# The opening and the close of a two-block transformer kernel rearranged: the conditioning row broadcast by TensorE, first chunk scaled from its bank, last sums by column halves

## The reference, cut to what matters

```
mods = silu(c) @ w_ada + b_ada               # nine rows of 1024: shift, scale, gate of three sublayers
n = rmsnorm(x, g_pre) * (1 + scale0) + shift0
f = (silu(n @ w_gate) * (n @ w_up)) @ w_down # D_FF = 2816, 22 blocks of 128 hidden units
h = x + 0.5 * gate0 * rmsnorm(f, g_post)
...                                          # attention, ffn1, second block with mlp0, MLA, mlp1
out = rms_norm(h + relu(hn @ w_up)**2 @ w_down, final_norm_g)
```

## Time and profile before

| | |
|---|---|
| time, median of 3 runs | 1213.88 us (1212.95 to 1217.24) |
| the profiled execution | 1212.7 us, its span 1211.4 us |
| PE busy | 1151.8 us, 95% of the span |
| DVE, ACT, POOL busy | 67%, 51%, 5% |
| mean granted PE clock | 0.988 |
| DMA | 231.75 MB, mean 191 GB/s |

### The profile page before, as it was taken

One profiled execution on the slowest core, in us unless ns is written; L12 is line 12 of the kernel. 1 busy time (PEld: TensorE's weight loads), 2 busy tenths in 40 slices (PEclk: granted clock), 3 DMA queues, 4 the chain that ended last, 5 costly groups with the idle time before them and its releaser, 6 DMA issues.

```text
span 1211.4 us, 19269 instructions
## 1 busy us (share of the span) xinstructions
PE 1151.8 (95%) x7570; PEld 1052.6 (87%) x7570; DVE 808.5 (67%) x1334; ACT 622.6 (51%) x1138; POOL 54.7 (5%) x75
## 2 busy tenths in 40 slices
PE   4999999899998999999999898999999889999998
PEld 4988899699987999999799778999998778899997
DVE  4878888777666756555768767565558666656555
ACT  5644444646656544444644455544556444554453
POOL 3100000000001000000012100000000100000000
PEclk9999999999999899999999899999999999999999
DMA  8969998373222566655352234555554413555540
GB/s 345 407 260 411 341 351 308 139 298 118 105 105 71 200 239 211 227 198 176 128 190 100 95 105 150 198 176 195 186 180 153 154 63 102 212 199 177 195 150 35
DMA packets 34009, 231.75 MB, mean 191 GB/s; under 512 B 3704, under 2 KB 5120, under 8 KB 6528
## 3 DMA queue, kind: packets, MB, share of 16 engines
q1 hardware_dynamic: 31952, 226.24, 51.2%
q10 hardware_dynamic: 1968, 4.29, 1.0%
HBM read 229.45 MB, written 1.06 MB: 190 GB/s over the span
## 4 chain that ended last, share of the span: by engine, by line
PE 77%; DVE 11%; ACT 8%; issue 2%; DMA 1%; POOL 1%; DVEq 0%; SPq 0%; ACTq 0%; POOLq 0%
PE ps L396 35%; PE pacc L396 34%; DVE wlo L359 4%; ACT whi L358 2%; PE ps L406 2%; PE ps L409 2%; ACT wk L1158 2%; PE pacc L406 1%; ACT arena L669 1%; POOL st L523 1%; DVE st L1153 1%; DVE tmp L711 1%; DMA raw<-in_stream 1%; DMA cst<-in_const 1%; PE pacc L409 1%
## 5 line engine op out<-in xcount | busy, mean ns | idle before, releaser
L359 DVE TENSOR_TENSOR wlo<-raw,whi 128x1024 fp32r<-128x1024 f32 x353 | 430.2, 1225 | 177.1 <-ACT whi L358 168.7
L358 ACT ACTIVATE whi<-raw 128x1024 fp32r<-128x1024 f32 x353 | 368.8, 1055 | 163.1 <-PE pacc L396 83.2
L396 PE MATMUL ps<-nhi,whi 128*128 128x256 f32 x1256 | 362.7, 289 | 2.6 <-DVE arena L1416 1.1
L396 PE MATMUL ps<-nlo,whi 128*128 128x256 f32 x1256 | 357.0, 284 | 0.0
L396 PE MATMUL ps<-nhi,wlo 128*128 128x256 f32 x1256 | 356.9, 284 | 0.0
L396 PEld LDWEIGHTS ps<-nhi,whi 128*128 128x128 f32 x1256 | 242.4, 193 | 8.5 <-DVE arena L1416 1.4
L396 PEld LDWEIGHTS ps<-nlo,whi 128*128 128x128 f32 x1256 | 242.4, 193 | 4.4 <-issue 0.5
L396 PEld LDWEIGHTS ps<-nhi,wlo 128*128 128x128 f32 x1256 | 242.3, 193 | 0.0
L879 ACT ACTIVATE sg<-ps 128x256 f32<-128x256 f32 x104 | 39.9, 384 | 165.2 <-PE ps L396 165.2
L396 PE MATMUL pacc<-whi,mhi 128*128 128x512 f32 x240 | 95.6, 398 | 0.0
L396 PE MATMUL pacc<-wlo,mhi 128*128 128x512 f32 x240 | 94.0, 392 | 0.0
(11 more groups left out here) (316 smaller groups left out, 1783.3 us busy)
## 6 DMA issues: line engine op xcount, KB each, us to landing
raw<-in_stream SPq DMA_DIRECT2D x213, 1024.0 KB, 4.9
gates<-in_g_post ACTq DMA_DIRECT2D x3, 512.0 KB, 7.4
h<-in_x SPq DMA_DIRECT2D x1, 1024.0 KB, 7.2
cst<-in_const ACTq DMA_DIRECT2D x1, 1024.0 KB, 4.8
arena<-bias_rows ACTq DMA_DIRECT2D x1, 1024.0 KB, 14.4
out<-tmp SPq DMA_DIRECT2D x4, 256.0 KB, 2.2
silu_c<-in_c_row ACTq DMA_DIRECT2D x1, 512.0 KB, 5.8
arena<-in_final_g SPq DMA_DIRECT2D x1, 512.0 KB, 3.8
```

Source lines behind the costliest of these rows:

```text
L358: t_hi = act.do(lambda e: e.activation(whi[:, s, :], src, ACT.Copy), arrived, room)
L359: t_lo = dve.do(lambda e: e.tensor_tensor(wlo[:, s, :], src, whi[:, s, :].bitcast(F32), ALU.subtract), arrived, room, t_hi)
L396: return e.matmul(o, lt[a], rh[b], start=start and first, stop=stop and last)
```

## The change

What it does, part by part. (1) `c` is loaded as one row of 4 KB on one partition; two products with a row of ones put it on 128 partitions in two banks, and ACT takes silu from there. The constants go to ACT's queue, ahead of the columns; x comes in two transfers. (2) ACT squares both halves of x ahead of silu, one `rstd` serves both, the diagonals are made on DVE. (3) 16 and 20 `busy` matmuls stand ahead of and behind the transposing products. These write the banks of `fix`, two chunks to a bank; chunk 0 is scaled by ACT directly from its bank, and the other seven are copied to `wk` (`rest_of_rows`) after the splits of fg0 and fu0. The blocks j = 0 to 3 begin in the banks of `ps`. (4) shift and scale of k = 0 are made on DVE, and the matmuls of k = 0 wait for each part by itself, in fours, the first parts first; for k = 1 to 7 their order is as before but hi by lo and lo by hi of weights and rows change places. (5) `last_units` takes i = 1 by f outside and n inside. `whole` puts `final(i, 0)` between the updates, and `final(i, 1)` ahead of `ends`; `write` multiplies one half on ACT and the other on DVE, and the two halves are stored from two queues.

```diff
@@ -318,15 +318,15 @@
             after = raw_free.get(2 * (n - NR), []) + raw_free.get(2 * (n - NR) + 1, [])
             sp.load(raw[:, n % NR, :], stream[n], s_raw[n % NR], 16 * (n // NR + 1), after)
-        s_cr, s_c, s_x, s_k, s_late, s_rel = sem("s_cr"), sem("s_c"), sem("s_x"), sem("s_k"), sem("s_late"), sem("s_rel")
-        t_c = act.load(silu_c[:, :], bass.AP(tensor=c_row.tensor, offset=c_row.offset, ap=[[0, P], [1, D]]), s_cr, 16)
+        s_cr, s_c, s_x, s_x1, s_k, s_late, s_rel = (sem("s_" + n) for n in ("cr", "c", "x", "x1", "k", "late", "rel"))
+        crow = arena[0:1, 6144:7168]
+        t_c = act.load(crow, c_row, s_cr, 16)
+        t_const = act.load(cst[:, 0:NEARLY], const[:, 0:NEARLY], s_k, 16)
+        t_x = [sp.load(h[:, 0, :], x[0:P, :], s_x, 16), sp.load(h[:, 1, :], x[P:T, :], s_x1, 16)]
         t_cols = act.load(cl[:, :], cols, s_c, 16)
-        t_x = sp.load(h[:, :, :], x.rearrange("(i p) d -> p i d", p=P), s_x, 16)
-        t_const = sp.load(cst[:, 0:NEARLY], const[:, 0:NEARLY], s_k, 16)
         for _ in range(NR):
             load_chunk()
-        t_silu = act.do(lambda e: e.activation(silu_c[:, :], silu_c[:, :], ACT.Silu), t_c)
         ada = {"n": {m: 0 for m in range(9)}, "done": {}}
         def ada_unit(m, src, arrived):
@@ -438,7 +438,7 @@
             units, meets, done = [], [], [[None, None], [None, None]]
-            order = [(n, i, f) for i in range(2) for n in range(LAST) for f in range(2)]
+            order = [(n, 0, f) for n in range(LAST) for f in range(2)] + [(n, 1, f) for f in range(2) for n in range(LAST)]
             if not cross.halves:
                 order = [(0, 0, 0), (0, 0, 1), (0, 1, 0), (0, 1, 1), (1, 0, 0), (1, 0, 1), (1, 1, 0), (2, 0, 0), (2, 0, 1),
                          (1, 1, 1), (2, 1, 0), (2, 1, 1)]
@@ -506,6 +506,7 @@
             return done
+        act.quiet(lambda e: e.preload_act_table(ACT.Silu))
         t_idr = act.do(lambda e: e.activation(identr[:, :], ident, ACT.Copy), t_const)
         pe.wait(t_const, t_idr)
         half = mod[:, 39:40]
@@ -584,20 +585,17 @@
                 banks.give(b, t2)
             parts.t[k] = [t1, t2]
-        def shifted_chunk(c, source, parts, scale, shift, *after, by_act=False):
-            o, tk, b = source
+        def shifted_chunk(c, source, parts, scale, shift, *after, by_act=False, lane=dve):
+            o, tk = source
             z = wk[:, 0:6, :].rearrange("p a b -> p (a b)")[:, c * T:(c + 1) * T]
             hi, lo = parts.hi[:, c, :], parts.lo[:, c, :]
             t = act.do(lambda e: e.activation(z, o, ACT.Identity, bias=shift, scale=scale), tk, *after)
-            if b is not None:
-                banks.give(b, t)
             if by_act:
                 t1 = act.do(lambda e: e.activation(hi, z, ACT.Copy), t)
             yield
             if not by_act:
                 t1 = dve.do(lambda e: e.tensor_copy(hi, z), t)
                 yield
-            lane = pool if by_act and c < 7 else dve
             t2 = lane.do(lambda e: e.tensor_tensor(lo, z, hi.bitcast(F32), ALU.subtract), t1)
             parts.t[c] = [t1, t2]
             yield
@@ -839,19 +837,19 @@
             def whole(self, i):
                 self.update(i, 0)
+                self.final(i, 0)
                 self.update(i, 1)
-                self.final(i, 0)
+                self.final(i, 1)
                 self.ends(i)
-                self.final(i, 1)
                 self.write(i)
             def write(self, i):
                 r, t = self.r[i]
-                for f in range(2):
-                    w = slice(f * 512, f * 512 + 512)
-                    to = dve.do(lambda e: e.tensor_scalar(tmp[:, i, w], tmp[:, i, w], r, None, ALU.mult), t,
-                                self.gated[i, f])
-                    sp.load(out[i * P:(i + 1) * P, w], tmp[:, i, w], s_o[2 * i + f], 16, to)
+                a, b = tmp[:, i, 0:512], tmp[:, i, 512:1024]
+                t0 = act.do(lambda e: e.activation(a, a, ACT.Copy, scale=r), t, self.gated[i, 0])
+                t1 = dve.do(lambda e: e.tensor_scalar(b, b, r, None, ALU.mult), t, self.gated[i, 1])
+                act.load(out[i * P:(i + 1) * P, 0:512], a, s_o[2 * i], 16, t0)
+                sp.load(out[i * P:(i + 1) * P, 512:1024], b, s_o[2 * i + 1], 16, t1)
             def first(self, done):
                 self.done[0] = done
@@ -959,55 +957,94 @@
         sh = [mod[:, 8:16], mod[:, 24:32]]
-        ts = []
+        ssq = new_stat(2)
         for i in range(2):
-            ssq = new_stat()
-            t = act.do(lambda e: e.activation(tmp[:, i, :], h[:, i, :], ACT.Square, accum_out=ssq), t_x)
-            r, t = rstd(ssq, D, EPS, t)
-            ts.append([act.do(lambda e: e.activation(dg[:, i, :], ident, ACT.Copy, scale=r), t, t_const)])
+            t_sq = act.do(lambda e: e.activation(tmp[:, i, :], h[:, i, :], ACT.Square, accum_out=ssq[:, i:i + 1]), t_x[i])
+        for f in range(2):
+            b, w = banks.take(), slice(f * 512, f * 512 + 512)
+            tk = put_last(b.ap, ones[0:1, :], crow[:, w], True, t_c)
+            t_silu = act.do(lambda e: e.activation(silu_c[:, w], b.ap, ACT.Silu), tk)
+            banks.give(b, t_silu)
+        busy(16)
         gain = mod[:, 40:48]
-        g_pre, b_scale = (cl[:, COLS[n] + a:COLS[n] + a + 8] for n, a in (("g_pre", 0), ("b_ada", 8)))
+        g_pre, b_shift, b_scale = (cl[:, COLS[n] + a:COLS[n] + a + 8] for n, a in (("g_pre", 0), ("b_ada", 0), ("b_ada", 8)))
         t_gain = dve.do(lambda e: e.scalar_tensor_tensor(gain, b_scale, 1.0, g_pre, ALU.add, ALU.mult), t_cols)
+        r, t = rstd(ssq, D, EPS, t_sq)
+        ts = [diagonal(i, r[:, i:i + 1], t) for i in range(2)]
         zs = []
-        open_fix()
-        for c, (b, tk) in enumerate(turn(h, 8, ts, True)):
-            z = wk[:, 0:6, :].rearrange("p a b -> p (a b)")[:, c * T:(c + 1) * T]
-            t = act.do(lambda e: e.activation(z, b.ap[:, 0:T], ACT.Copy), tk)
-            banks.give(b, t)
-            zs.append((z, t, None))
-        close_fix()
-        held = fix + [banks.take() for _ in range(4)]
-        made = []
-        for k in range(8):
-            feed(4 * k + 2)
+        for c in range(8):
+            for i in range(2):
+                o = fix[c // 2].ap[:, (c % 2) * T + i * P:(c % 2) * T + i * P + P]
+                tk = pe.do(lambda e: e.matmul(o, h[:, i, c * P:(c + 1) * P], dg[:, i, :], start=True, stop=True), ts[i])
+            zs.append((fix[c // 2].ap[:, (c % 2) * T:(c % 2) * T + T], tk))
+        dg_free[0] = dg_free[1] = [tk]
+        zs = [(o, zs[c | 1][1]) for c, (o, _) in enumerate(zs)]
+        busy(20)
+        held = [banks.take() for _ in range(4)] + fix
+        def first_columns():
+            t_shift = dve.do(lambda e: e.tensor_tensor(sh[0][:, 0:1], adac[:, 0:1], b_shift[:, 0:1], ALU.add),
+                             ada["done"][0, 0], t_cols)
+            t_scale = dve.do(lambda e: e.scalar_tensor_tensor(sc[0][:, 0:1], adac[:, 8:9], g_pre[:, 0:1], gain[:, 0:1],
+                                                              ALU.mult, ALU.add), ada["done"][1, 0], t_gain)
+            return t_shift, t_scale
+        def columns(k):
             t_shift = act.do(lambda e: e.activation(sh[0][:, k:k + 1], adac[:, k:k + 1], ACT.Identity,
                                                     bias=col("b_ada", k)), ada["done"][0, k], t_cols)
             t_scale = act.do(lambda e: e.activation(sc[0][:, k:k + 1], adac[:, 8 + k:9 + k], ACT.Identity,
                                                     bias=gain[:, k:k + 1], scale=col("g_pre", k)),
                              ada["done"][1, k], t_gain)
-            for _ in shifted_chunk(k, zs[k], n1, sc[0][:, k:k + 1], sh[0][:, k:k + 1], t_shift, t_scale, by_act=True):
+            return t_shift, t_scale
+        def rest_of_rows():
+            for c in range(1, 8):
+                o, tk = zs[c]
+                z = wk[:, 0:6, :].rearrange("p a b -> p (a b)")[:, c * T:(c + 1) * T]
+                t = act.do(lambda e: e.activation(z, o, ACT.Copy), tk)
+                fix[c // 2].free = [t]
+                zs[c] = (z, t)
+        by_column = [[(j, n) for n in range(2) for j in range(8)]] * 7 + [[(j, n) for j in range(8) for n in range(2)]]
+        by_column[0] = [(j, n) for a in (0, 4) for n in range(2) for j in range(a, a + 4)]
+        made = []
+        for k in range(8):
+            feed(4 * k + 2)
+            t_shift, t_scale = columns(k) if k else first_columns()
+            for _ in shifted_chunk(k, zs[k], n1, sc[0][:, k:k + 1], sh[0][:, k:k + 1], t_shift, t_scale, by_act=True,
+                                   lane=pool if 0 < k < 7 else dve):
                 pass
             feed(4 * k + 4)
+            if k == 0:
+                rest_of_rows()
             units = [Unit(("ffn0_fg", k)), Unit(("ffn0_fu", k))]
-            for j, n in ([(j, n) for n in range(2) for j in range(8)] if k < 7 else
```

(41 more changed lines are left out.)

## The result

The changed kernel took 1216.01 us in the median of 20 runs (1213.70 to 1220.32), the kernel before 1213.91 in 20 runs beside it (1211.81 to 1217.24). The ratio is 1.0018, its interval 1.0010 to 1.0027: some 2 us slower, where 1212.0 was forecast and 1208.0 to 1215.2 given as the range. The median lies outside the range, and the sign is the other one. The profiled execution took 1214.37 us, its span 1213.1, 1.7 more than that of before.

The account below looks back on a forecast made before the run. PE was busy for 95% of the span, so only its waits and slow stretches could pay. From the median 1213.9: opening - 3.9, low clock + 1.3, end + 0.7, giving 1212.0 us; range 1208.0 to 1215.2.

Parts of the forecast that it names:

- the 2.6 us of the opening: Opening's net gain: 3.9 us from an earlier k = 1 and vanished later waits, less 1.3 for a low clock.
- the first down matmul at about 67.5, not 70.3: Sign expected in the changed trace: PE's first down matmul at about 67.5 us instead of 70.3.
- k = 0 near 17.0: Opening on PE: k = 0 starts near 17.0 us (19.6 with late constants), 4.5 us sooner than before.
- k = 1 near 26.0, behind a gap: Opening: k = 1, held by chunk 5 and then nlo, starts at 26.0 instead of 28.69, after PE idles from about 22.8.
- slack of 3 us: Opening: the matmuls of k = 0 in fours have 3 us of slack and cost nothing.
- The low clock between k = 0 and k = 1, 1.3 us: PE's idle gap ahead of k = 1 lowers the clock afterwards, costing 1.3 us; bounds nothing and 3.0.
- The waits of k = 2 and 3, 1.25 us, gone: Opening: later chunks come 3 us or more sooner, so 1.25 us of PE waits at k = 2 and 3 vanish.
- The end, + 0.7: Kernel's end: final between the updates adds 0.94 us, side by side multiplications save 0.25; bounds 0.3 and 3.1.
- The crossings, 0: New order of i = 1 in last_units: no effect, with 0.3 us either way for each of three crossings.
- (d): Rival, slower: the close costs more than the opening earns, through the store from ACT's queue adding 2.4; 1214.4 us, chance 0.07.

Follow-up runs that it names:

- e1: Changed kernel with the bank order as before (blocks 0 to 3 in the banks of fix): 1213.09 us, ratio to the kernel before 0.9990.
- e2: Kernel before with only the new bank order (blocks 0 to 3 in ps, 4 to 7 in fix): 1218.78 us, ratio 1.0045.
- e7: e1 with the row of c repeated over the partitions by DMA, without the products with ones: 1212.60 us, ratio to the kernel before 0.9993.
- e6: e1 without both calls of busy (16 and 20) in the opening: 1210.05 us, ratio to the kernel before 0.9969.
- e3: Changed kernel with the old end and the old order of i = 1 in last_units: 1216.93 us, ratio to the kernel before 1.0025.
- e4: Kernel before with the new end and the new order of i = 1 in last_units: 1213.92 us, ratio 1.0002.
- e8: e1 without the second call, busy(20), keeping busy(16): 1212.03 us, ratio to the kernel before 0.9986.
- e5: e1 with the end's two updates one behind the other again, final behind them: 1212.56 us, ratio to the kernel before 0.9991.

## Why the prediction was wrong, point by point

- **The step that failed is the sum, where the 2.6 us of the opening were carried from k = 7 to the end as they were** ("the first down matmul at about 67.5, not 70.3"). The part "blocks j = 0 to 3 begin in the banks of `ps`" was described as an edit and never priced. It has a price 45 us later: the down products sum in `pacc`, and wait for `hm` of blocks 4 and 5. The hidden parts come from DVE and ACT one in 1.24 us, so four blocks later in that queue means 5 us later. In numbers: the first down product starts at 72.24, before at 70.33, + 1.9. Up to the second group of down products (84.91, before 83.19) two waits of before fall away (0.68 and 0.45 us idle) and the slow clock costs 1.3, together - 0.2: + 1.7. Shown by e1 and e2. That the spans of the two profiles differ by 1.7 as well is chance: ACT's split at 364.0 before is 1.6 later here and the one at 405.6 only 0.3, because between them lies a stretch of low clock that was shorter here (mean granted clock 0.76 from 396 to 403, before 0.53 from 394 to 401); at DVE's first update of the end it is 1.4 (1202.12, before 1200.69), and the end adds 0.25.
- **k = 0 near 17.0**: wrong, it was 21.1. Three terms were mis-sized, because PE kept its slow pace until 17.0. From start to start the two products of a single row took 3.67 us, where the sum has about 2; 16 `busy` 3.48, not 2.6; the transposing products 5.26, not 3.9.
- **k = 1 near 26.0, behind a gap**: 26.93, with no gap. That the size is nearly right is luck. Chunk 5 was there one us sooner than the sum has it (21.1, not 22.1; the repeated row costs the chunks 1.9 us by e7 and e1, not 1.2), and it wasn't what ACT's split of fg2 waited for: `busy(16)` had held the whole chain for longer. e6 parts the two. The cover that I named for k = 0 ("slack of 3 us") wasn't there, it was used up by `busy`. With k = 1 of before at 28.81, the slow clock of k = 0 had cost 1.56 us and not 1.44, the later waits 1.13 and not 1.25; their sum is the same.
- **The low clock between k = 0 and k = 1, 1.3 us**: it didn't come, for there was no gap; the price came at another one, ahead of the down products, at 1.3 us. The rule of the Trainium skill cited above ("TensorE: Matmul & The Clock Gate", "HAM oscillation — how this bites in real kernels") held there: 4.5 us of idle PE, and the clock was low behind it, here and in e2. Behind the 1.13 us of e6 it stayed high.
- **The waits of k = 2 and 3, 1.25 us, gone**: mostly right, 0.3 us of 1.2 is left. The opening's 2.75 at k = 7 is near my 3.9 - 1.3 = 2.6 by luck: k = 1 gave 1.9 and not 2.7, the later waits 0.9, and the low clock took nothing.
- **The end, + 0.7**: the sign right, the size + 0.25. DVE's first delay was as worked out (the second update 0.65 later), but POOL's power fell from 0.93 to 0.54 us twice, since `final` no longer ran on DVE beside it.
- **The crossings, 0**: e3 and e4 show nothing of them. **Rivals**: (d) had the right sign for the wrong reason; the store from ACT's queue costs 0.3 to 0.5, not 2.4. Where I looked for what comes next on DMA and the clock, it was on the banks.

Open: whether the difference between e1's 1.2 us in the median and the 2.0 of its trace is more than spread; its interval holds both, and how often a stretch of low clock falls into an execution changes its time by more than that. And what the 16 and the 20 `busy` each cost in time is taken from e8 and e6, whose medians lie 2.0 us apart; no run leaves out the 16 alone.

## What to carry to other kernels

When accumulators change places, look for the next writer of each bank and for the order in which its last readers run; the price stands there, not where the change is. A head start is worth what the next shared resource lets through: follow it to the first join behind the edited stretch before adding it to the end. And products that only keep an engine warm stand in its queue like any others; leave them out once before believing in them (here that was worth 2.6 us at the first down product, and the ratio to before went from 0.9990 to 0.9969).

## What the runs showed of the hardware

- In the opening PE goes at half the pace at first, and neither the products of a single row nor `busy(16)` changed that. By windows of half a microsecond the changed kernel starts 4 or 5 matmuls in each until 17.0 and 6 or 7 from there, with PE at work from 6.46 on, over 10 us before; the four of the single row took 3.75 us. e7 has no products of a single row, starts at 8.94 with `busy(16)` and is fast from 17.6 on. In the kernel before PE starts at 11.15 with the transposing products and is fast from 15.0 on; in e6, without `busy`, from 14.0 on. Counted from the first transposing product, the fast pace came after 2.9 to 5.1 us in all twelve traces, whatever PE had done ahead of it. Why the products ahead of it didn't bring the pace up, no run shows.
- The granted clock of the windows says 1.00 in all of these stretches, but the first record of it in each trace starts only where the pace rises (17.19, before 14.83, e6 13.85). Ahead of the first record the pace is the reading.
- The row of c repeated over the partitions (512 KB) put the first six chunks behind it 1.9 us later (the first at 10.61 in e7, 8.75 in e1; chunk 5 at 23.1 and 21.2).
- POOL's power on one column took 0.54 us alone, and 0.92 or 0.93 while DVE ran a 512 column instruction of two SBUF operands (e1 and e5 differ in just that), in all twelve traces, to 0.01 us.
- The time of one and the same program goes with its mean granted clock: the changed kernel's runs at 0.992 or above took 1213.7 to 1214.4 us, those at 0.985 or below 1217.3 to 1220.3. So 2 us of a change must be looked for in the trace, and only many runs tell them in the time.
